# The last norm of a hybrid decoder step: GpSimd adds the shift, VectorE keeps the multiplication

## What is computed

```python
def _layernorm(x, g, b):
    mu = x.mean(-1, keepdims=True)
    var = jnp.mean(jnp.square(x - mu), -1, keepdims=True)
    return (x - mu) * lax.rsqrt(var + LN_EPS) * g + b
xp = _layernorm(ALPHA * xp + _moe(xp, ...), ln_g[layer, 1], ln_b[layer, 1])
```

## Time and profile before

| what | value |
|---|---|
| median of three runs | 1265.58 us (1265.21 to 1266.97) |
| profiled execution | 1265.74 us, of which the span is 1263.9 us |
| PE busy | 1089.5 us (86% of the span) |
| DVE busy | 517.6 us (41%) |
| ACT busy | 302.9 us (24%) |
| POOL busy | 112.5 us (9%) |

### The profile page before, as it was taken

The page is one execution under the profiler, slowest core; times in us unless marked ns, Lnnn a source line. Parts: engine busy times, 40 slices in busy tenths (PEclk is TensorE's granted clock), DMA queues, the critical chain, the costliest instruction groups (busy, mean ns, idle before and its releaser), DMA issues.

```text
span 1263.9 us, 19022 instructions
## 1 busy us (share of the span) xinstructions
PE 1089.5 (86%) x7162; PEld 667.3 (53%) x7162; DVE 517.6 (41%) x1330; ACT 302.9 (24%) x691; POOL 112.5 (9%) x152
## 2 busy tenths in 40 slices
PE   7999994799999189999899998999999379999910
PEld 3686452444444056777788875555554244444400
DVE  2570345111111553488545556666334511111155
ACT  0102123111111222323334331455312211111111
POOL 0010003000000300000211111210000300000030
PEclk9999996799999689999999997999999689999965
DMA  9568009899992632132322242854500989999251
GB/s 355 199 244 157 1 5 357 321 364 359 377 352 110 222 128 100 34 100 76 91 74 74 74 133 76 318 191 156 200 34 18 356 314 375 361 367 353 103 199 66
DMA packets 85380, 246.28 MB, mean 195 GB/s; under 512 B 9488, under 2 KB 50496, under 8 KB 66720
## 3 DMA queue, kind: packets, MB, share of 16 engines
q1 hardware_dynamic: 63584, 150.53, 33.9%
q0 software_dynamic: 17088, 77.64, 16.7%
q10 hardware_dynamic: 4608, 16.78, 3.4%
HBM read 205.63 MB, written 58.16 MB: 209 GB/s over the span
## 4 chain that ended last, share of the span: by engine, by line
PE 83%; DVE 8%; issue 4%; DMA 3%; ACT 1%; POOL 1%; POOLq 0%; DVEq 0%; SPq 0%; ACTq 0%
PE bank L1212 18%; PE bank L1148 10%; PE bank L1232 9%; PE bank L1358 8%; PE bank L1282 5%; PE bank L1455 4%; PE bank L1300 3%; PE bank L1202 2%; PE bank L1332 2%; DVE acc L2271 2%; DVE stat L2065 1%; PE bank L1708 1%; PE bank L1733 1%; PE bank L1162 1%; PE bank L1139 1%
## 5 line engine op out<-in xcount | busy, mean ns | idle before, releaser
L1148 PE MATMUL bank<-ring,cat 128*128 128x512 f32 (+1 forms) x320 | 141.0, 594 | 1.3 <-ACT cat L1851 1.3
L1212 PE MATMUL bank<-ring,work 128*128 128x512 f32 x256 | 114.7, 600 | 0.0
L1358 PE MATMUL bank<-xT,ring 128*128 128x288 f32 x448 | 110.9, 407 | 0.0
L2251 DVE TENSOR_TENSOR work<-work,bank 128x256 f32<-128x256 f32 x32 | 13.5, 421 | 219.5 <-ACT work L1830 219.5
L1358 PEld LDWEIGHTS bank<-xT,ring 128*128 128x128 f32 x448 | 84.6, 190 | 24.1 <-issue 1.5
L1148 PEld LDWEIGHTS bank<-ring,cat 128*128 128x128 f32 (+1 forms) x320 | 56.0, 179 | 74.0 <-issue 73.9
L1212 PEld LDWEIGHTS bank<-ring,work 128*128 128x128 f32 x256 | 48.3, 194 | 54.7 <-issue 54.7
L1282 PE MATMUL bank<-xT,ring 128*128 128x288 f32 x256 | 63.1, 407 | 0.0
L1830 ACT ACTIVATE work<-bank 128x256 f32<-128x256 f32 x32 | 12.3, 384 | 208.3 <-PE bank L1212 208.3
L1202 PE MATMUL bank<-const,work 128*128 128x128 f32 x256 | 36.4, 291 | 29.3 <-DMA work<-xrows 29.3
L1232 PE MATMUL bank<-ring,work 128*128 128x512 f32 x128 | 57.7, 593 | 1.0 <-issue 1.0
(11 more groups left out here) (426 smaller groups left out, 1865.7 us busy)
## 6 DMA issues: line engine op xcount, KB each, us to landing
ring<-in_stream_dram SPq DMA_DIRECT2D x71, 1024.0 KB, 7.4
cat<-in_stream_dram SPq DMA_DIRECT2D x16, 1024.0 KB, 9.0
work<-xrows ACTq DMA_DIRECT2D x32, 512.0 KB, 5.6
xT<-in_stream_dram SPq DMA_DIRECT2D x16, 1024.0 KB, 9.0
work<-in_stream_dram SPq DMA_DIRECT2D x16, 1024.0 KB, 10.5
yrows<-work POOLq DMA_DIRECT2D x32, 512.0 KB, 9.2
by_batch<-in_pages_dram SPq DMA_DIRECT2D x128, 128.0 KB, 2.4
xrows<-work POOLq DMA_DIRECT2D x1, 8192.0 KB, 27.4
```

The lines of the kernel that those rows point to most:

```text
L1148: i = pe.matmul(bank(n)[0:ROWS[tile], :], cat[:, k, tok(tile)], slot(w[k // 4], 4, 512)[:, k % 4, :], start=(k == 0), stop=(k == KC - 1))
L1212: i = pe.matmul(bank(n), xgT[:, e % 2, k, :], sparse_slot(layer, 3 * e + k // 4, 4, 512)[:, k % 4, :], start=(k == 0), stop=(k == KC - 1))
L1358: i = pe.matmul(bank(n + s)[:, 0:nn], slot(w, KC, 256)[:, k, P * (m % 2):P * (m % 2) + P], xT[:, k, a:a + nn], start=(k == 0), stop=(k == ...
```

## The change

In the last norm alone (k equal to 3) DVE's multiplication raises a new semaphore, `gain_applied`, and `affine` returns: DVE neither waits for the multiplication nor adds the shift. POOL waits for `gain_applied` of the tile, adds the shift with one `tensor_tensor` over the tile, which raises `ln_done`, waits for that, and stores the tile as before. The three earlier norms are unchanged.

```diff
--- before.py
+++ after.py
@@ -537,6 +537,7 @@
         ln_affine = sem("ln_affine")
         ln_scaled = sem("ln_scaled")
         ln_done = sem("ln_done")
+        gain_applied = sem("gain_applied")
         stored = sem("stored")
         pooled_ready = sem("pooled_ready")
         vn_var = sem("vn_var")
@@ -1121,6 +1122,9 @@
             ln_params(3)
             pool_mixture(1)
             for tile in range(NT):
+                r = ROWS[tile]
+                pool.wait_ge(gain_applied, tile + 1)
+                pool.tensor_tensor(x[0:r, tile, :], x[0:r, tile, :], lnp[0:r, D_MODEL:], ALU.add).then_inc(ln_done, 1)
                 pool.wait_ge(ln_done, (2 * LAYERS - 1) * NT + tile + 1)
                 store(pool, outs["x"][:, D_MODEL * tile:D_MODEL * tile + D_MODEL], x[:, tile, :])
             pool.wait_ge(stored, 16 * n_stores[0])
@@ -2079,7 +2083,11 @@
                 i, r = NT * k + tile, ROWS[tile]
                 dve.wait_ge(ln_loaded, 16 * (k + 1))
                 dve.wait_ge(ln_scaled, i + 1)
-                step(dve.tensor_tensor(x[0:r, tile, :], x[0:r, tile, :], lnp[0:r, 0:D_MODEL], ALU.mult))
+                i = dve.tensor_tensor(x[0:r, tile, :], x[0:r, tile, :], lnp[0:r, 0:D_MODEL], ALU.mult)
+                if k == 2 * LAYERS - 1:
+                    i.then_inc(gain_applied, 1)
+                    return
+                step(i)
                 dve.tensor_tensor(x[0:r, tile, :], x[0:r, tile, :], lnp[0:r, D_MODEL:], ALU.add).then_inc(ln_done, 1)
 
             def add_output(layer, half, tile):
```

## The result

The changed kernel takes 1270.26 us (median of six runs, 1269.52 to 1270.73) against 1265.28 for the kernel before in the six runs beside it: ratio 1.004, 95% interval 1.0029 to 1.005. The forecast was 1270.4. The profiled execution took 1269.96 us, with a span of 1268.2 us.

What follows compares the result with a forecast made beforehand. The prediction took DVE to bound the tail; three periods longer by 0.92 us gave 2.76, and with the last tile the store came 4.82 us later, so 1270.4 us (0.38% slower), range 1263.8 less 0.4 to 1272.5.

Steps and rivals of the forecast that it cites:

- What bounds the tail: Last norm: DVE sets the pace, busy 33.9 of 37.5 us; the 11.4 us after the last store's issue stay unchanged.
- The gain per tile: DVE's cycle in the last norm: without the shift, the reciprocal follows the factor, saving 1.26 us per tile.
- The addition: POOL's new 128x1024 shift addition in the last norm: A taken as 2.29 us, bounds 1.89 and 2.91.
- The hold: DVE's scale operation, two SBUF operands, stands until POOL's addition ends, as at 790.47; period 6.95 to 7.87 us; chance 0.42.
- rival 1: Last norm: the scale operation slips through and the first combination stands instead; store 2.8 us late, 1268.4 us; chance 0.32.
- Rival 2: Last norm: POOL waits until both combinations are through and adds beside the statistics; 1.8 us faster, 1263.8 us; chance 0.11.
- rival 3: Last norm: no blocking that matters, two-operand reads go side by side; store 3.65 us early, 1261.9 us; chance 0.10.
- Hops: Waits around POOL's addition: 0.08 us from DVE's end to its start, 0.30 us from its end to the store.
- The sum: Last store issued 4.82 us later than 1251.99, at 1256.81; generally at 1245.36 + 5A.
- POOL's reconfiguration: Before POOL's first addition: 0.24 us elsewhere in the trace, delaying it by at most some 1 us; taken as nothing.

Runs made afterwards that it cites:

- e4: Changed kernel with the shift not added at all in the last norm, GpSimd waiting only for the factor before it stores; 1259.13 us, ratio 0.9963.
- e1: Changed kernel with the small scale operation written as tensor_scalar, the reciprocal as pointer scalar, so one SBUF tensor operand; 1266.92 us, ratio 1.0021.
- e8: Changed kernel with GpSimd waiting, ahead of its addition, also for the first of the two combinations behind the factor; 1266.18 us, a single run.
- e2: Changed kernel with GpSimd waiting, ahead of each addition, also for the end of both combinations behind the factor; 1265.62 us, ratio 1.0005.
- e5: Changed kernel with each last-norm factor put ahead of the next tile's statistics, and DVE adding the last tile's shift; 1261.87 us, ratio 0.9987.
- e6: As e5, and the small scale operation has one tensor operand, as in e1; 1262.04 us, ratio 0.9973 to the kernel before.

## Why the prediction was right

- **What bounds the tail**: right. The chain runs over DVE, held four times, up to the last scale operation, then over ACT's write, the last factor and POOL's last addition. From the first combination to the first factor it is 9.20 us before and 9.22 after, and behind the last store's issue 11.9 and 12.0.
- **The gain per tile, 1.26 us**: right. e4 has a period of 5.69, as 6.95 - 1.26.
- **The addition, A = 2.29 us**: 2.33 measured. Line 1011 was the right row to go by, with both operands read without repetition; line 1020 would have given 1.89 and a forecast 2 us lower. (The sum in the prediction gives 2.28; it then used 2.29.) Half as many partitions took 2.33 as well, and half the columns 1.25.
- **The hold**: right in kind and in the operation that it meets. The scale operation was due 0.03 us behind POOL and came 0.02 us behind. That was a narrow call, and it was worth 1.86 us (e1), about what lay between the forecast and rival 1 (2.0). It ended 0.02 us after POOL's addition, not 0.08 as in the earlier trace rows. There the prediction did not use its own reading: for rivals 1 and 2 it let a held operation end at POOL's end plus 0.08 plus its own length minus 0.23, which for one of 0.16 us is 0.01. The prediction also says that without the Trainium skill's rule rival 3 would be the sum; but the hold was already in its own row at 790.47.
- **Hops**: 0.09 for 0.08 ahead of the addition, 0.29 to 0.30 for 0.30 behind it.
- **The sum**: 4.82 us later forecast, 4.84 measured in the tail. The match of the last tenths is luck: five times 0.04 us for A add 0.2, and the scale operation that ends 0.06 us sooner at four tiles takes 0.24 away. So is the match of the medians, 1270.4 against 1270.26, in six runs that lie up to 1.2 us apart; the profiled execution took 1269.96 where the sum gave 1270.56.
- **Rival 2** would have needed POOL to come second. e8 shows that POOL does wait then, and e2, that its addition is free beside the statistics. The rival also took it that the fourth tile's scale operation isn't held. In e2 and e8 it took 2.33 us, so the rival's gain of 1.8 us was not there: the tail is 0.33 us longer than before's in e2 and 0.53 us shorter in e8. **Rival 3**, no blocking, is excluded by the changed kernel's period, 7.86 us where the rival had 5.69; e4 has 5.69, but only without the addition.
- **POOL's reconfiguration**: none was seen to cost anything; the first addition started 0.09 us after the factor like the others.

Open is how the hold is granted when both come due within some hundredths of a microsecond. Here POOL was ahead by 0.01 to 0.02 us in all four meetings, and no profile has it the other way round. Nor does any run have a GpSimd addition that reads no SBUF, so whether its reads or its writes hold VectorE is not told apart here.

## What to carry to other kernels

Before work is moved from VectorE to GpSimd, list what VectorE issues during the time that GpSimd will need, and count the SBUF tensors that each of those operations reads. With two, VectorE stands for about the rest of GpSimd's operation, here 2.2 us for 1.26 us saved; with one (e1, e2, e5, e6), or one and another in PSUM, it wasn't held. So put the hand-over ahead of statistics, reductions or other one-tensor work, and leave the last piece, with nothing beside it, to the faster engine: from the last factor's start to the last store it is 2.77 us with VectorE's addition (e5) and 3.93 with GpSimd's (after). A one-element operation can carry the whole delay, and a pointer scalar in place of a second tensor freed it in e1 and e6.

## What the runs showed of the hardware

- The recorded length of an operation includes the time for which it is held, on both engines: a scale operation of one element reads 2.33 us (0.16 alone), an addition on GpSimd 3.37 us (2.33 alone). Neither shows as idle time: the changed kernel's list of DVE's waits in the tail has three, of 10.3, 1.4 and 0.3 us, for a gather and for ACT.
- A held operation loses less than the overlap. It ended 0.13 to 0.15 us sooner than if it had begun at the other's recorded end: the scale operation of after at 1227.32, not 1227.46; e2's factor at 1232.09, not 1232.24; e8's addition at 1231.46, not 1231.59. In e6 combinations that started 0.19 to 0.20 us before the addition ended were longer by 0.02 us at most.
- POOL's gathers do not hold DVE so: before's first two combinations took 2.61 us with the gather of 1216.10 to 1217.19 among them, and 2.60 at 1226.96 with no gather beside them.
- The `tensor_scalar` with a pointer scalar took 0.21 us where the `scalar_tensor_tensor` took 0.16.
